# The odd mixer as one stage of ten weight units, with its state space tables computed in the feed-forward stage ahead

## What is computed

```python
z = h @ w_in                                    # 1024 -> 1024
zc, zd = z[..., :512], z[..., 512:]
# pool half: windowed means over 2, 4, 8, 16 tokens, minus zc, then a 128x128 product per group
y_c = einsum('bsgc,gcd->bsgd', pooled - zg, pool_w) * pool_scale
# state space half: 32 groups of 16 channels with 64 complex states each
lam_bar = exp(lam * dt);  b_bar = (lam_bar - 1) / lam * b
states[t] = lam_bar * states[t-1] + b_bar @ u[t]
y = gelu((c @ states).real + d * u)
ab = y @ w_glu                                  # 512 -> 1024
y_d = ab[..., :512] * sigmoid(ab[..., 512:])
x = x + concat([y_c, y_d]) @ w_out              # 1024 -> 1024
```

## Time and profile before

| what | value |
| --- | --- |
| median of 3 runs | 3704.47 us (3703.61 to 3710.2) |
| the profiled execution, its own time | 3706.94 us |
| its span, first to last instruction | 3705.1 us |
| TensorE busy | 3306.9 us, 89% |
| VectorE busy | 2269.8 us, 61% |
| ScalarE busy | 1812.0 us, 49% |
| GpSimd busy | 207.1 us, 6% |
| mean granted TensorE clock | 0.931 of full |

### The profile page before, as it was taken

One profiled execution on the slowest core, in us unless ns is written; L12 is line 12 of the kernel. 1 busy time (PEld: TensorE's weight loads), 2 busy tenths in 40 slices (PEclk: granted clock), 3 DMA queues, 4 the chain that ended last, 5 costly groups with the idle time before them and its releaser, 6 DMA issues. The chain is left out here.

```text
span 3705.1 us, 59466 instructions
## 1 busy us (share of the span) xinstructions
PE 3306.9 (89%) x23344; PEld 3035.2 (82%) x23344; DVE 2269.8 (61%) x2572; ACT 1812.0 (49%) x2255; POOL 207.1 (6%) x115
## 2 busy tenths in 40 slices
PE   6997689999379979898899898987899999999997
PEld 6996479898248979897899798986799889999995
DVE  3441345546864456665645566645588888888885
ACT  3441343444014434546334355552677777777773
POOL 0000100001130011101100111100000000000000
PEclk9995589999679989999999999997999999999999
DMA  4540045454014544342445433333699999999993
GB/s 160 182 178 35 1 168 184 159 186 174 6 57 174 189 156 145 117 144 99 167 168 184 137 127 131 130 116 114 229 344 348 344 343 343 343 344 343 346 341 129
DMA packets 97334, 702.36 MB, mean 190 GB/s; under 512 B 10913, under 2 KB 11041, under 8 KB 13473
## 3 DMA queue, kind: packets, MB, share of 16 engines
q1 hardware_dynamic: 97184, 700.26, 51.6%
HBM read 699.16 MB, written 1.05 MB: 189 GB/s over the span
## 5 line engine op out<-in xcount | busy, mean ns | idle before, releaser
L803 PE MATMUL ps<-act_high,weight_low 128*128 128x256 f32 x3152 | 902.2, 286 | 0.0
L803 PE MATMUL ps<-act_high,weight_high 128*128 128x256 f32 x2768 | 802.0, 290 | 48.2 <-DVE act_low L424 22.5
L803 PE MATMUL ps<-act_low,weight_high 128*128 128x256 f32 x2768 | 793.7, 287 | 0.0
L803 PE MATMUL ps<-weight_low,act_high 128*128 128x256 f32 x2432 | 691.6, 284 | 0.0
L803 PE MATMUL ps<-weight_high,act_high 128*128 128x256 f32 x2272 | 658.5, 290 | 28.0 <-DVE weight_low L879 10.6
L803 PE MATMUL ps<-weight_high,act_low 128*128 128x256 f32 x2272 | 645.8, 284 | 0.0
L803 PEld LDWEIGHTS ps<-act_high,weight_low 128*128 128x128 f32 x3152 | 616.0, 195 | 0.0
L803 PEld LDWEIGHTS ps<-act_high,weight_high 128*128 128x128 f32 x2768 | 542.3, 196 | 59.9 <-DVE act_low L424 20.2
L803 PEld LDWEIGHTS ps<-act_low,weight_high 128*128 128x128 f32 x2768 | 542.6, 196 | 2.1
L803 PEld LDWEIGHTS ps<-weight_low,act_high 128*128 128x128 f32 x2432 | 470.4, 193 | 4.7 <-issue 1.0
L803 PEld LDWEIGHTS ps<-weight_high,act_high 128*128 128x128 f32 x2272 | 439.4, 193 | 38.8 <-issue 26.5
(11 more groups left out here) (422 smaller groups left out, 5274.3 us busy)
## 6 DMA issues: line engine op xcount, KB each, us to landing
ring<-in_l_w_in SPq DMA_DIRECT2D x90, 1024.0 KB, 4.8
ring<-in_l_moe_up SPq DMA_DIRECT2D x56, 1024.0 KB, 6.0
ring_more<-in_l_moe_gate SPq DMA_DIRECT2D x56, 1024.0 KB, 5.0
ring_more<-in_l_moe_up SPq DMA_DIRECT2D x56, 1024.0 KB, 6.1
vtm<-in_l_moe_down SPq DMA_DIRECT2D x56, 1024.0 KB, 4.9
ring<-in_l_ffn_up SPq DMA_DIRECT2D x55, 1024.0 KB, 4.8
merged<-in_l_moe_gate SPq DMA_DIRECT2D x55, 1024.0 KB, 4.9
ring<-in_l_moe_down SPq DMA_DIRECT2D x55, 1024.0 KB, 4.9
```

Source lines behind the costliest of these rows:

```text
L803: ins = nc.tensor.matmul(out, still[a], moving[b], start=first and n == 0, stop=last and n == 2, skip_group_check=True)
```

## The change

The odd mixer becomes one block, `odd_stage`, with ten units of 1 MB: 0 to 3 are `w_in` (the state space half first), 4 and 5 (`AN`) are the rows of `w_out` for the pool half, 6 and 7 the two halves of `w_glu` (value and gate, each 512 columns wide), 8 and 9 (`BN`) the rows of `w_out` for the state space half. Unit 0 stands ahead of the state space loop; units 1 to 5 are put between its steps on TensorE by the table `INSERTED`, the pool's matmuls at steps 8 and 9; units 6 to 9 follow the loop. Two half products of `w_glu` with 512 columns take the place of four with 256.

The tables move to the third feed-forward stage: `StateTables.vector` is a generator that hands out its work in twenty pieces, two per step, between VectorE's `make_low` calls. That stage is unrolled: no hardware loop on any engine. The sines on ScalarE go into its second step. The load of the mixer's input table moves from the third feed-forward stage to the second. Three raw buffers are used in the mixer in place of two, and their first order is changed.

```diff
-    def stream(eng, start, body, end):
+    def stream(eng, start, body, end, unrolled=False):
         start()
-        with eng.Fori(0, G // 2) as i:
-            for odd in range(2):
-                body(Step(i, odd))
+        if unrolled:
+            for n in range(G - 1):
+                body(Step(n // 2, n % 2))
+        else:
+            with eng.Fori(0, G // 2) as i:
+                for odd in range(2):
+                    body(Step(i, odd))
         end()
...
                 silus(t.n + 1)
                 make_high(t.unit(3), t.unit(3)[0] * 2 + mb)
+                if aside is not None and t.n == 1:
+                    aside.scalar(act)
...
                 hidden_lows(t.n, t.odd)
                 make_low(t.unit(1))
+                if aside is not None:
+                    next(pieces, None)
                 make_low(t.unit(2))
                 products(t.n + 1)
                 make_low(t.unit(3))
+                if aside is not None:
+                    next(pieces, None)
...
+INSERTED = {0: 1, 3: 2, 6: 3, 11: 4, 13: 5}
+POOLED, MIXED = 8, 9
...
+            norm.tensor(pe)
+            project(0)
             drive(0)
             drive(1)
             for n in range(NT):
+                unit = INSERTED.get(n)
+                if unit is not None and unit < AN:
+                    project(unit)
+                elif unit is not None:
+                    out(unit, 6 if unit == AN else 0)
+                if n == POOLED:
+                    pool_sums()
+                if n == MIXED:
+                    pool_mix()
                 if n + 2 < NT:
                     drive(n + 2)
                 readout_of(n)
+            glu(GATE, 2)
+            glu(VALUE, 6)
+            out(BN, 0)
+            out(BN + 1, 2)
...
+            norm.scalar_start(act)
+            make_high(1)
+            norm.scalar(act)
+            for n in range(4):
+                unload(n)
+                make_high(n + 2)
+            for i in range(2):
+                pool_take(i)
+            for i in range(4):
+                pool_split(i)
+            gelu(0)
+            make_high(GATE)
+            make_high(VALUE)
+            gelu(1)
+            make_high(BN)
+            act.wait_ge(made.sem, made.base + GATE + 1)
+            nc.scalar.activation(gate, ps[:, 2:4, :].rearrange("p b (a t) -> p (b a) t", a=2), ACT.Sigmoid)\
+                .then_inc(taken.sem, 1)
+            for i in range(2):
+                glu_split(i)
+            make_high(BN + 1)
...
+            norm.vector(dve)
+            make_low(1)
+            for n in range(NT):
+                rotate_and_scan(n)
+                if n in (0, 3, 6, 9):
+                    make_low(2 + n // 3)
+                if n == 11:
+                    make_y(0)
+                    for i in range(4):
+                        pool_split(i)
+                if n == 13:
+                    y_split(0)
+                    add_x(AN, 6)
+                    make_low(GATE)
+                if n == 15:
+                    add_x(AN + 1, 0)
+                    make_low(VALUE)
+            make_y(1)
+            y_split(1)
+            make_low(BN)
+            for i in range(2):
+                glu_product(i)
+            for i in range(2):
+                glu_split(i)
+            make_low(BN + 1)
+            add_x(BN, 0)
+            ahead.vector(dve, high.base + ODD_UNITS + 1)
+            add_x(BN + 1, 2)
...
-        tables = [(t[:, 0:3618], d["l_even_tables"]), None, (t[:, 0:4664], d["l_odd_tables"]),
+        tables = [(t[:, 0:3618], d["l_even_tables"]), (t[:, 0:4664], d["l_odd_tables"]), None,
```

More of the change, by code:

```diff
@@ L660, in end @@
                 first_root(c)
-            stream(act, start, triple, end)
+            stream(act, start, triple, end, aside is not None)
         @block.vector
@@ L1429 @@
 CH = 32
[L1432 to L1460, removed]
-    for s in (pooled, taken, mixed):
-        s.advance(4)
@@ L1616, in drive @@
             def drive(n):
+                if n in (0, 8):
+                    pe.wait_ge(taken.sem, taken.base + n // 8 + 1)
                 if n >= 2:
@@ L1660, in _, with make_y @@
                 last.then_inc(scanned.sem, 1)
-            for m in range(4):
-                dve.wait_ge(read.sem, read.base + 4 * m + 4)
-                nc.vector.scalar_tensor_tensor(out=y[:, m, :], in0=u[:, m, :], scalar=skip[:, m:m + 1], in1=ps[:, 4 + m, 0:T],
-                                               op0=ALU.mult, op1=ALU.add).then_inc(skipped.sem, 1)
+            def make_y(i):
+                dve.wait_ge(read.sem, read.base + 8 * i + 8)
+                for m in (2 * i, 2 * i + 1):
+                    last = nc.vector.scalar_tensor_tensor(out=y[:, m, :], in0=u[:, m, :], scalar=skip[:, m:m + 1],
+                                                          in1=read_of(m), op0=ALU.mult, op1=ALU.add)
+                last.then_inc(y_made.sem, 1)
@@ new lines, in glu_product, with glu_split @@
+            def glu_product(i):
+                dve.wait_ge(taken.sem, taken.base + 5)
+                dve.wait_ge(made.sem, made.base + VALUE + 1)
+                nc.vector.tensor_tensor(pair(g, i), one(6 + i), pair(gate, i), ALU.mult).then_inc(glu_made.sem, 1)
+            def glu_split(i):
+                dve.wait_ge(glu_high.sem, glu_high.base + i + 1)
+                nc.vector.tensor_tensor(c.act_low[:, 4 + 2 * i:6 + 2 * i, :], pair(g, i),
+                                        c.act_high[:, 4 + 2 * i:6 + 2 * i, :].bitcast(F32), ALU.subtract).then_inc(glu_low.sem, 1)
@@ new lines, in odd_stage, with __init__ @@
+    taken.advance(5)
+    for s in (taken_dve, pool_high, pool_low, added):
+        s.advance(4)
+    for s in (y_made, y_high, y_low, pooled, pool_taken, mixed, glu_made, glu_high, glu_low):
+        s.advance(2)
+    norm.advance()
+class OddTables:
+    def __init__(self, c):
+        t, seg = c.tables, c.seg
+        flat = lambda m: m.rearrange("p a b -> p (a b)")
+        self.operators = t[:, 0:2048].rearrange("p (g t s) -> p g t s", g=4, t=TT)
+        self.weights = t[:, 2048:2560].rearrange("p (g d) -> p g d", g=4)
+        self.scale, self.skip = t[:, 2560:2564], t[:, 2564:2568]
+        self.lam = [t[:, 2568 + NT * n:2568 + NT * n + NT] for n in range(3)]
+        self.b_in = t[:, 2616:3640].rearrange("p (r m s) -> p r m s", r=2, m=4)
+        self.c_out = [t[:, 3640 + 512 * n:4152 + 512 * n].rearrange("p (n c) -> p n c", n=NT) for n in range(2)]
+        self.decay = t[:, 4664:4664 + NT]
+        self.phases = [flat(m).rearrange("p (n t) -> p n t", n=NT) for m in (seg[:, 0:16], seg[:, 16:32])]
+        self.readout = flat(c.merged[:, 0:6]).rearrange("p (m n) -> p m n", m=3)
@@ L1723 @@
+def odd_mixer(c):
+    d, o = c.dram, OddTables(c)
+    odd_stage(c, Rms(c, c.gains[:, 4 * KD:5 * KD]), [d["l_odd_units"][n] for n in range(ODD_UNITS)], o.operators, o.weights,
+              o.scale, o.b_in, o.decay, o.phases, o.readout, o.skip,
+              then=[d[n][d[n].shape[0] // 4 * 3] for n in ("l_ffn_gate", "l_ffn_up")])
 RET_HEADS = 4
```

334 lines of the change are left out of this document (241 added, 93 removed).

## The result

The changed kernel takes 3627.16 us (median of 4 runs, 3624.22 to 3630.67), the kernel before 3704.04 us beside it (4 runs, 3703.04 to 3710.2): ratio 0.9788, interval 0.9776 to 0.9799, so 77 us less. Predicted were 3621, with a range of 3609 to 3648. The profiled execution is the one of 3624.22 us, with a span of 3622.4; for it the sum had said 3623.7.

What follows compares the result with a forecast made beforehand. Feed-forward stages were taken as bound by TensorE, the mixer by VectorE. Mixer -92.1, pieces +5.5, clock +3.4 make -83.2 against 3706.94: 3623.7; the median, 2.5 lower, gives 3621 us, range 3609 to 3648 with rivals.

Steps and rivals of the forecast that it cites:

- the clock's term: Mixer loop: two of five inserted units start at the slow clock, 3.4 us in all, between 0 and 8.5.
- VectorE waits for `drive` under 1 us: Sign in the mixer loop: drives behind inserted units come 0.7 to 0.9 us late, taken back by up to 1.04.
- the bound of 5: Mixer loop: late drives behind all five inserted units cost at most some 5 us; no stall was summed.
- Piece 9: Third feed-forward stage: table piece of 6.6 us, 1.7 over what its slot hides.
- piece 10: Third feed-forward stage: table piece of 6.8 us, adding 1.8 us of stall with VectorE still behind.
- piece 11: Third feed-forward stage: table piece of 5.4 us, adding 1.9 us of stall; VectorE catches up from piece 12.
- no other: Sign in the third feed-forward stage: TensorE waits for `weight_low` in the fifth and sixth steps only; stage 5 us longer.
- GpSimd first: Rival, mixer: six `make_low` in and after the loop wait for GpSimd, 1.5 us each, +9: 3630 us; 15%.
- Slow clock throughout: Rival, mixer loop: each inserted unit runs at 1.2 GHz, +25 us: 3646 us; 13%.
- It doesn't overlap: Rival, mixer loop: inserted units hold up the drives in full, 28 us: 3649 us; 5%.
- Pieces cost twenty more: Rival, third feed-forward stage: small table operations hold up `make_low` in many steps: 3641 us; 4%.
- slower through instruction supply: Rival, unrolled feed-forward stage: instructions supplied too slowly; at 0.1 us per matmul 3741 us; 2%.

Runs made afterwards that it cites:

- even cut: Changed kernel with the same table work cut into pieces by time, none in the last slot: 3622.62 us, ratio 0.977.
- two edits: Two kernels, each against the changed one: `drive(n + 2)` ahead of the inserted unit, 3625.73 us; unit 7's `make_low` after the second `y_split`, 3624.63 us.
- the three edits: Changed kernel with tables cut by time, drives ahead of inserted units and unit 7's `make_low` later, together: 3616.7 us, in a second run 3615.87 us.

## Why the prediction was right, point by point

**What bounds it.** Right for the mixer: VectorE sets its pace up to the loop's end, but for four waits, and TensorE behind it. (TensorE was not busy in all the rest of the span, as I had read: the strip of before has 7 and 6 in its fourth and fifth slices. Nothing in the sum hangs on it.) The account from the first matmul of unit 0 (911.99) to the last addition (1039.79):

| term | predicted | measured | read from |
| --- | --- | --- | --- |
| to the first rotation | 8.3 | 8.8 | 920.79 |
| sixteen steps and all put between them | 84.2 | 84.9 | 1005.72 |
| tail up to the last readout | 7.0 | 7.9 | `w_glu` at 1013.62 |
| two `w_glu` units | 11.5 | 12.1 | product at 1025.71 |
| gate products, `w_out` units, last addition | 13.7 | 14.1 | 1039.79 |
| sum | 124.7 | 127.8 | |

The 3.1 us too many are close to the clock's term, 3.4: -92.1 + 3.4 = -88.7, measured -88.85 from norm to norm. That is in part luck. Of the 3.1 us the clock's share can be read for the last readout only (3.22 for 1.91, so 1.3); the rest is spread over the other rows, up to 0.7 us each. And 3.4 was itself mis-worked: 33 matmuls where 44 would go are 5 x 11/44 = 1.25 us lost, not 1.7, so two slow starts would have been 2.5.

**The clock: size near, place wrong.** The failed step is that two of five inserted units begin slow, at 1.7 us each. None does. Unit 2 starts at 941.47 and the drive behind it at 947.42, 5.95 us later, and units 1 and 3 take the same; units 4 and 5 take 5.62 and 5.69 us in the same way. That is 0.15 to 0.22 above the prices of 5.75 and 5.47 for each. It is the stretch ahead of the unit that is slow, when TensorE has only drives and readouts. TensorE from 935.92, and then the last readout:

```profile
935.92 2.07 PE L1718 MATMUL ps<-vtm,tables 32*128 32x256 f32 x4
937.92 3.62 PE L1728 MATMUL ps<-rowbuf,merged 128*32 128x256 f32 x8
...
947.42 1.13 PE L1718 MATMUL ps<-vtm,tables 32*128 32x256 f32 x4
...
1010.47 3.22 PE L1728 MATMUL ps<-rowbuf,merged 128*32 128x256 f32 x8 [4.62 <-POOL rowbuf L1929]
```

The readout ahead of unit 2 takes 3.62 us instead of 1.9, the last one 3.22. At the full clock a readout takes 1.91; the windows show 0.56 and 0.66 granted.

**The late drives: mechanism right, size off.** The failed step is "VectorE waits for `drive` under 1 us". For step 3 I had counted from VectorE's start (934.92): readout done at 4.75, unit at 10.5, drive at 11.6, wanted at 10.9, so 0.7 late. Measured: readout done at 6.6 (941.5), drive at 13.6 (948.5), wanted at 11.0 (948.58 less 2.69), so 2.69 late. Nearly all of the 2.0 us is the slow readout. The other long one, 2.46 at 990.63, is no such loss. Unit 4 started at 5.74 after the step's start (said: 5.6) and the next step began at 12.5 (said: 12.1); but VectorE was there at 10.1 and not at 11.2, because step 12 skipped its wait for GpSimd (0.42 us for the last rotation operation). GpSimd had finished its pair under `pool_split`. So a wait that the profile calls 2.46 cost 1.3 against the count, and 1.07 of that came back in step 13. That a late step skips its wait for GpSimd holds in full at the two long waits and in the larger part at the two short ones (0.66 and 0.73 us for the operation that waits); with it the loop of 84.9 us is 0.7 above the sum without any stall, in spite of 6.8 us of waits. That shows how much less a wait can be worth than its row says. Drives put first cut 3.9 us from the loop, within the bound of 5 that I had given.

**The tables in the feed-forward stage: sum right by luck, parts off.** 5.5 us were predicted for the pieces, and the stage is 5.8 longer. But that is 7.3 us for the pieces (205.60 - 198.31) less the 1.5 by which the unrolled stage is shorter than the looped one, a term put at nothing. Piece 9 cost 2.39 (said 1.7), piece 10 0.97 (1.8), piece 11 1.67 (1.9); these three are 5.0 instead of 5.4. The failed step is "no other" wait: the last piece, one operation of 2.29 us, stands ahead of the last `hidden_lows`, on which TensorE waits there, 1.68 us. In that last step no further unit is behind, so there is no slack of 2.50 us in it as in the earlier trace rows; I had taken each slot's slack from the steady step. The even cut shows both: with all of it away the stage takes 6.7 us less.

**Costs put at nothing.** The sines cost nothing to speak of: the stage of the even pieces has them and takes 198.89 us, 0.6 more than the unrolled one without tables. The input table's load in its new place cost 0.15 us (200.57 and 200.42 for the second stage), within the noise. Unrolled code came with 1.45 us less.

**The rivals.** *GpSimd first* is refuted: behind steps 0, 3, 6 and 9 `make_low` started about 0.16 us ahead of GpSimd (924.10 and 924.26) and GpSimd's pair took 4.5 us in place of 2.7. Behind steps 13 and 15 a small VectorE operation was first and `make_low` came later, in 15 between GpSimd's two operations (1005.88, 1006.90, 1007.11) as I had put it. The Trainium skill, SBUF — State Buffer, section "SBUF: two separate sides", has the one that starts first keep the ports for its whole instruction, with the other blocked. The rows agree as far as they go: 2.27 us for `make_low`, so not delayed, and 1.8 to 2.0 us more for GpSimd's pair. GpSimd ahead of VectorE happened with the small rotation operation alone (1.42 us for 0.42). *Slow clock throughout* is refuted by five units at full pace. *It doesn't overlap* is refuted by the kernel with the units ahead of the loop, which needs 10.4 us more up to the last step for three units. *Pieces cost twenty more* is refuted by the 7.3 us, *slower through instruction supply* by the unrolled stage without pieces.

**The 6 us between 3621 and 3627.16.** I took the median as 2.5 below the profiled execution, as in the kernel before. Here the profiled one is the fastest of four, 2.9 below the median. The sum itself was 0.5 us off (3623.7 and 3624.22), closer than its parts deserve, as said above; that a profiled execution stands the same way to its median in two kernels was the weak step. Executions of one kernel spread by up to 7 us.

## What to carry to other kernels

Count a merge of stages queue by queue from the old trace, per step, and let each late step give back the wait that it skips: here the sum for the loop came within a microsecond though the profile now lists 6.8 us of new waits. Work that is handed out in pieces beside a bound engine costs only where a piece is longer than its slot, so cut by time and look at the last step apart. Compare a changed stage with one that differs in nothing else: against the looped stage the pieces seemed to cost 5.8 us, against the unrolled one 7.3. When an edit removes waits of TensorE, compare the clock behind them, in more than one execution, before believing or rejecting it: two edits that had won 2.7 and 2.9 us by the end of the loop's tail showed 0.4 each in the profiled mixer, and 3.5 together, while their medians were 3.3 and 4.4 us lower.

## What the runs showed of the hardware

- In the loop, with drives and readouts only and waits of TensorE of 1.0 to 1.7 us between them, the granted clock fell to 0.56 (934 to 939) and eight readout matmuls took 3.62 us in place of 1.91. Over the weight unit behind it (941.5 to 947.4) it was 1.00.
- The time from L1866 to the norm went with the order of work in the loop: 26.6 to 27.0 us in the five profiled executions that have the changed kernel's loop (both of itself, even pieces, and the two with tables in the mixer), 28.2 to 29.1 in the six of the five kernels with an edit in the loop or its tail. The clock behind the loop differs in the windows; why it does is open.
- With ten products of zeros with 32 rows, 2.33 us in a gap (and twenty in the loop), the 5 us behind the last readout were at the full clock (1.00 in 1001 to 1006); without them they were at 0.87 (1002 to 1007 in the first run of the three edits).
- 120 unrolled matmuls a step ran no slower than in a hardware loop (198.31 and 199.76 us for the stage).
